# Silu read straight from PSUM for two gates of a hybrid decoder layer, one buffer doubled, one wait dropped, and all engine orders planned anew

## The reference

```python
h = rmsnorm(x, norm_g[l]) * (1.0 + scale[:, None, :]) + shift[:, None, :]
z = h @ w_in[l]
xr, gr, q, k, v, ga, qi, ki, wi = jnp.split(z, split_points, axis=-1)
xr = causal_depthwise_conv(xr, conv_w[l], conv_b[l])
y_r = rg_lru(xr, lru_wx[l], lru_bx[l], lru_wa[l], lru_ba[l], lru_a[l]) * jax.nn.silu(gr)
y_a = dsa_attention(q.reshape(B, S, N_HEADS, HEAD_DIM), k, v,
                    qi.reshape(B, S, N_IDX_HEADS, IDX_DIM), ki, wi) * jax.nn.silu(ga)
y = jnp.concatenate([y_r, y_a], axis=-1) @ w_out[l]
x = x + gate[:, None, :] * y
```

## Time and profile before

| | us |
|---|---|
| median of 3 runs | 636.92 |
| lowest, highest | 636.62, 640.52 |
| the profiled execution, device time | 639.16 |
| its span in the trace | 637.4 |
| PE busy | 540.3 (85%) |
| DVE busy | 444.1 (70%) |
| ACT busy | 374.0 (59%) |
| POOL busy | 247.5 (39%) |

### The profile page before, as it was taken

How to read it: one execution, slowest core, us unless ns; L and a number is a source line. 1 busy time by engine, 2 the same in 40 slices (tenths; PEclk the granted TensorE clock), 3 DMA queues, 4 the chain that set the end, 5 groups by cost and what they waited for, 6 DMA issues and landing times. The chain is left out here.

```text
span 637.4 us, 8051 instructions
## 1 busy us (share of the span) xinstructions
PE 540.3 (85%) x2676; PEld 447.9 (70%) x2676; DVE 444.1 (70%) x996; ACT 374.0 (59%) x678; POOL 247.5 (39%) x207
## 2 busy tenths in 40 slices
PE   2369989979999996999999406478999999999994
PEld 2356868768777773888777305467888999988873
DVE  5985467767998978945778988856456665665532
ACT  7423236544698989865789334464556675656631
POOL 5050853252525466277656400750223030304322
PEclk9859989999999999899999855559999999999999
DMA  8966460341021121035450420030010001011011
GB/s 344 411 204 230 103 152 11 99 100 32 2 66 34 34 64 35 2 99 133 117 148 2 171 93 0 0 99 2 1 67 34 33 2 67 23 45 67 0 67 66
DMA packets 16457, 51.96 MB, mean 82 GB/s; under 512 B 4000, under 2 KB 5024, under 8 KB 15392
## 3 DMA queue, kind: packets, MB, share of 16 engines
q1 hardware_dynamic: 16416, 51.45, 25.6%
HBM read 37.81 MB, written 4.19 MB: 66 GB/s over the span
## 5 line engine op out<-in xcount | busy, mean ns | idle before, releaser
L1384 PE MATMUL pair<-h_hi,w_hi 128*128 128x512 f32 (+1 forms) x352 | 115.7, 411 | 7.7 <-DVE rnn_gr L1187 4.8
L1384 PE MATMUL pair<-h_lo,w_hi 128*128 128x512 f32 (+1 forms) x352 | 111.1, 397 | 0.0
L1384 PE MATMUL pair<-h_hi,w_lo 128*128 128x512 f32 (+1 forms) x352 | 110.1, 394 | 0.0
L1309 DVE TENSOR_TENSOR pt_lo<-pair,pt_hi 128x512 fp32r<-128x512 f32 (+3 forms) x96 | 50.5, 553 | 70.6 <-ACT pt_hi L968 70.2
L863 ACT ACTIVATE bias_sb<-score_sb,tinies 128x1024 bf16<-128x1024 f32 (+2 forms) x93 | 95.7, 1033 | 2.5 <-DVE tinies L1114 2.3
L1384 PEld LDWEIGHTS pair<-h_hi,w_hi 128*128 128x128 f32 (+1 forms) x352 | 65.7, 191 | 25.9 <-issue 13.8
L692 POOL TENSOR_SCALAR w_hi<-w_raw 128x1024 fp32r<-128x1024 f32 (+1 forms) x22 | 26.9, 1223 | 137.8 <-PE pair L1384 122.1
L1384 PEld LDWEIGHTS pair<-h_lo,w_hi 128*128 128x128 f32 (+1 forms) x352 | 66.8, 190 | 16.0 <-issue 1.1
L1384 PEld LDWEIGHTS pair<-h_hi,w_lo 128*128 128x128 f32 (+1 forms) x352 | 66.6, 189 | 15.7 <-issue 0.8
L1100 DVE TENSOR_SCALAR_CACHE_REDUCE bias_sb<-score_sb,tinies 128x640 bf16<-128x640 f32 (+2 forms) x93 | 72.5, 801 | 0.9
L782 POOL TENSOR_TENSOR x_res<-q_free,x_res 128x512 f32<-128x512 f32 x14 | 18.2, 1297 | 120.3 <-DVE q_free L1280 120.3
(11 more groups left out here) (199 smaller groups left out, 1258.9 us busy)
## 6 DMA issues: line engine op xcount, KB each, us to landing
w_raw<-in_w_tiles SPq DMA_DIRECT2D x21, 512.0 KB, 3.6
ada<-in_ada_w SPq DMA_DIRECT2D x8, 1024.0 KB, 18.1
x_sb<-in_x SPq DMA_DIRECT2D x8, 512.0 KB, 6.7
ada_g<-in_ada_w SPq DMA_DIRECT2D x8, 512.0 KB, 4.5
qs<-half_hi SPq DMA_DIRECT2D x16, 256.0 KB, 3.6
qs<-half_lo SPq DMA_DIRECT2D x16, 256.0 KB, 4.4
wo_raw<-in_w_out SPq DMA_DIRECT2D x8, 512.0 KB, 6.7
x_res<-in_x SPq DMA_DIRECT2D x8, 512.0 KB, 3.4
```

The source lines that it names most:

```text
L1309: nc.vector.tensor_tensor(pt_lo[:, 4 * b:4 * b + nc4, hh, :], psum[use % 2][:, 0:nc4 * P].rearrange("p (c q) -> p c q", q=P), f32(pt_hi[:, ...
L1384: ins = nc.tensor.matmul(psum[banks[half]][0:width, :], w[b][:, k, 0:width], hh[:, k, half * HALF:(half + 1) * HALF], start=(k == 0 and p ...
```

## The change

Six edits. (1) `silu(gr)`: one ACT instruction Silu from PSUM into a buffer `gr0` or `gr1` by turns; `tg` and DVE's `grm` are gone, and what waited for `grm` (the PE tile two later, POOL's `yr`) waits for the ACT instruction. (2) `silu(ga)`: one ACT instruction instead of two on ACT and three on POOL. (3) The read-out of q tiles no longer waits for the stacking DMAs of the tile before; POOL, which then fills the buffers that these DMAs read, still waits. The read-out of q0 no longer waits for the gate's bias. (4) Read-outs into `raw`, and the gate bias DMA, wait for the last DVE step of the recurrence instead of POOL's last `yr`. (5) The costs of the planner and its rule for activation tables. (6) Hence new orders on all engines; the multiset of the other instructions is unchanged.

```diff
-COUNT_A_US = (1.35, 1.25, 1.15)
+COUNT_A_US = (1.38, 1.27, 1.16)
...
+UPDATE_LAG = 0.8
+TABLE = {"silu": "silu", "sig": "sigmoid", "decay": "sigmoid", "root": "sqrt"}
...
-            add("ACT", ("silu", c), 2.4, 2, done, ("grm", c - 1) if c else ("gacc", KC - 1))
-            add("DVE", ("grm", c), 1.3, 2, ("silu", c), *prev)
+            add("ACT", ("silu", c), 1.1, 2, done, ("yr", c - 2) if c >= 2 else ("gacc", KC - 1))
...
-                if kind == "ga":
-
-                    link(nc.gpsimd.tensor_scalar(raw[:, :], raw[:, :], 0.5, 0.5, ALU.mult, ALU.add))
-                    nc.gpsimd.tensor_tensor(ga[:, n, 0:HALF], ga[:, n, 0:HALF], raw[:, 0:HALF], ALU.mult)
-                    nc.gpsimd.tensor_tensor(ga[:, n, HALF:], ga[:, n, HALF:], raw[:, HALF:], ALU.mult).then_inc(ga_ok, 1)
...
-                    pool.wait_ge(grm_ok, ct + 1)
-                    nc.gpsimd.tensor_tensor(yr[:, ct, :], yr[:, ct, :], rnn["gr"][:, :], ALU.mult).then_inc(rnn_done, 1)
+                    pool.wait_ge(silu_ok, ct + 1)
+                    nc.gpsimd.tensor_tensor(yr[:, ct, :], yr[:, ct, :], rnn[f"gr{ct % 2}"][:, :], ALU.mult).then_inc(rnn_done, 1)
...
                     if kind == "q" and n == 0:
                         act.wait_ge(v_ps, 1)
-                        act.wait_ge(gate_ok, 1)
                 if kind in RAW_KINDS and J["gr", 0] < j:
+                    act.wait_ge(rnn_dve, 5 * CT)
+                if kind == "ga":
                     act.wait_ge(rnn_done, CT)
                 if kind == "kv":
                     act.wait_ge(slot_done, IDX_SLOTS)
-                if kind in ("qi", "q"):
+                if kind == "qi":
                     act.wait_ge(stacked, 64 * QS.index(j))
...
-                    nc.scalar.activation(ga[:, n, :], src[:, :], ACT.Copy)
-                    ins = nc.scalar.activation(raw[:, :], src[:, :], ACT.Tanh, scale=0.5)
+                    ins = nc.scalar.activation(ga[:, n, :], src[:, :], ACT.Silu)
...
-                    if o[1]:
-                        act.wait_ge(grm_ok, o[1])
+                    if o[1] >= 2:
+                        act.wait_ge(rnn_done, o[1] - 1)
                     else:
                         act.wait_ge(gacc_ok, KC)
-                    nc.scalar.activation(tg, pairs[J["gr", o[1]] % 2][:, :], ACT.Sigmoid).then_inc(silu_ok, 1)
+                    nc.scalar.activation(rnn[f"gr{o[1] % 2}"][:, :], pairs[J["gr", o[1]] % 2][:, :], ACT.Silu).then_inc(silu_ok, 1)
...
-                    nc.vector.tensor_tensor(rnn["gr"][:, :], pairs[J["gr", ct] % 2][:, :], tg, ALU.mult).then_inc(grm_ok, 1)
...
-                            pe.wait_ge(grm_ok, ct + 1)
+                            pe.wait_ge(silu_ok, ct + 1)
```

More of the change, by code:

```diff
@@ L80 @@
 BIAS_OFF = {i: sum(keys_of(t) for t in range(i)) for i in range(NT)}
-RAW_KINDS = ("kiwi", "qi", "ga", "kv", "q")
+RAW_KINDS = ("kiwi", "qi", "kv", "q")
 RAW_USE = [j for j, t in enumerate(TILES) if t[0] in RAW_KINDS]
 EVAC = {j: n for n, j in enumerate(j for j, t in enumerate(TILES) if t[0] not in ("xr", "gr"))}
-HALVES = [j for j in RAW_USE if TILES[j][0] != "ga"]
 QS = [j for j in RAW_USE if TILES[j][0] in ("qi", "q")]
@@ L138, in stages @@
                     before = TILES[j - 2][:2]
-                    need.append({"xr": ("conv", before[1], 3), "gr": ("grm", before[1])}.get(before[0], ("evac", j - 2)))
+                    need.append({"xr": ("conv", before[1], 3), "gr": ("silu", before[1])}.get(before[0], ("evac", j - 2)))
             if j or k:
@@ L143, in stages @@
         done = (("kstep", j, STEPS[j] - 1), 0.2)
-        rnn_free = [("yr", c) for c in range(CT) if J["gr", c] < j]
+        rnn_free = [("rnn", c, 4) for c in range(CT) if J["gr", c] < j]
         if kind not in ("xr", "gr"):
@@ L156, in stages @@
                 need.append(("idx", len(UNITS) - 1))
-            add("ACT", ("evac", j), {"gate": 1.05, "kv": 3.1, "q": 1.05}.get(kind, 2.1), 3, *need)
+            if kind == "ga":
+                need.append(("yr", CT - 1))
+            add("ACT", ("evac", j), {"gate": 1.05, "kv": 3.1, "q": 1.05, "ga": 1.05}.get(kind, 2.1), 3, *need)
             need = [("evac", j)]
@@ L164, in stages @@
                 need.append(("vlo",))
-            add("POOL", ("after", j), {"ga": 3.7, "qi": 2.7, "q": 3.9}.get(kind, 2.4), 3, *need)
+            if kind != "ga":
+                add("POOL", ("after", j), {"qi": 2.7, "q": 3.8}.get(kind, 2.45), 3, *need)
         if kind in ("kiwi", "kv"):
@@ L187, in stages @@
             add("ACT", ("decay", c), 3.7, 2, (("sig", c, 1), 0.0), *([("rnn", c - 1, 4)] if c else []))
-            add("ACT", ("root", c), 2.4, 2, (("decay", c), 0.0))
-            for step, (us, after) in enumerate(((1.3, [("root", c)]), (1.3, [("root", c)]), (0.8, []), (1.3, [("pool_gx", c)]), (2.3, []))):
+            add("ACT", ("root", c), 1.15, 2, (("decay", c), 0.0))
+            for step, (us, after) in enumerate(((1.3, [("root", c)]), (1.3, [("root", c)]), (0.8, []), (1.3, [(("pool_gx", c), 0.3)]), (2.4, []))):
                 add("DVE", ("rnn", c, step), us, 3, *after, *([(("rnn", c, step - 1), 0.1)] if step else []))
-            add("POOL", ("yr", c), 2.5, 2, ("rnn", c, 4), ("grm", c))
+            add("POOL", ("yr", c), 2.5, 2, ("rnn", c, 4), ("silu", c))
     for w in range(NW):
@@ L229, in stages @@
             add("ACT", ("count_a", it, c), COUNT_A_US[c], 6, ("sign",), *([("update", it - 1, c)] if it else []))
-            add("DVE", ("update", it, c), UPDATE_US, 1, ("count_a", it, c), ("prep",))
+            add("DVE", ("update", it, c), UPDATE_US, 1, (("count_a", it, c), UPDATE_LAG), ("prep",))
         for c in range(3):
@@ L248, in stages @@
     slots = []
+    table = [""]
     todo = list(work)
@@ L266, in stages @@
         engine, us = work[event][:2]
+        if event[0] in TABLE or event[0] == "evac" and TILES[event[1]][0] == "ga":
+            us += 1.3 * (table[0] != TABLE.get(event[0], "silu"))
+            table[0] = {"decay": "exp"}.get(event[0], TABLE.get(event[0], "silu"))
         end[event] = free[engine] = start + us
@@ L418, in layer_kernel @@
         rnn = {}
-        for n, name in enumerate(("gr", "xc", "th")):
+        for n, name in enumerate(("gr0", "xc", "th", "gr1")):
             rnn[name] = sb("rnn_" + name, R_GA + 4096 * n, [P, S])
-        tg = sb("tg", R_GA + 12288, [P, S])[:, :]
         for n, name in enumerate(("gx", "a", "s")):
@@ L517, in layer_kernel @@
         silu_ok = sem("silu_ok")
-        grm_ok = sem("grm_ok")
         gx_ok = sem("gx_ok")
@@ L639, in _ @@
             sp.wait_ge(bias_ok, len(PICK))
-            sp.wait_ge(ga_ok, 4)
+            sp.wait_ge(halves_ok, len(RAW_USE))
+            sp.wait_ge(evac_done, len(EVAC))
             for ti in range(2):
@@ L822, in evacuate @@
                     if r:
-                        last = RAW_USE[r - 1]
-                        if TILES[last][0] == "ga":
-                            act.wait_ge(ga_ok, TILES[last][1] + 1)
-                        else:
-                            act.wait_ge(halves_ok, HALVES.index(last) + 1)
+                        act.wait_ge(halves_ok, r)
                     if kind == "qi" and n == 0:
```

20 lines of the change are left out of this document (7 added, 13 removed).

## The result

| | before | after |
|---|---|---|
| median of the runs timed side by side | 637.83 us | 620.73 us |
| lowest to highest | 636.62 to 640.52 | 619.93 to 621.56 |
| profiled execution, and its span | 639.16, 637.4 | 619.93, 618.1 |

The changed kernel takes 0.9726 of the time of the one before, with an interval of 0.969 to 0.9763. The forecast was 618.4 with a range of 614 to 626, so the time fell into the range, 2.3 us above the forecast. The span of the profiled execution came out at 618.1 where 617.9 had been worked out.

A forecast was written before the change was run, and what follows sets the result against it. DVE's own counts were taken to bound the phase before the loop, PE next. own_thr 19.5 us earlier took 639.16 to 619.7, less 2.2 for the median gave 617.4, plus 1 for waits 618.4; range 614 to 626.

The forecast's parts named there:

- What bounds: Before the loop: DVE's own counts end the phase, late through waits for ACT; without these and grm, own_thr at 338.3.
- TensorE: PE from gate0 to the projection's end: kv0 does not wait, k-steps take 1.36 us, end at 345.9 instead of 357.68.
- ACT and DVE up to kv0: At ct 3: square root ends at 257.2, eight counts bring ACT to 265.4, kv0 is read out until 268.5.
- The q tiles: POOL waits for stacking DMAs instead of ACT; splits at 283, 293.6, 304.2; costs ACT 1 to 3 us at q2, q3.
- The tail: End of the search: ga2 at 335.0, eight counts 8.2 us plus 0.3, post 5.8, own_thr at 353.3 instead of 372.79.
- Lock-step (A): Search rounds on ACT and DVE: each waits for the other, nothing overlaps, time 625.5 us; 15 in 100.
- ACT dearer (B): On ACT: table switches or Silu cost twice their rows, time 622 to 623 us; 8 in 100.
- POOL's wait (C): Stacking waits hold POOL's slab splits, so PE waits: 643 us and more, 3 in 100; 631 to 643, 4 in 100.
- (D): Loop's start: search ends earlier but w_out or the clock holds the start, 624 to 631 us; 3 in 100.

The follow-up runs named there:

- e7: Kernel before the change, ordered with planner costs set to the intervals seen in the trace; 631.8 us, ratio 0.9889.
- e10: Changed kernel with ga tiles done as before (copy and tanh on ACT, sigmoid and product on POOL), planned with matching costs; 623.2 us, ratio 0.9763.
- e8: Changed kernel with one gr buffer instead of two, the planner told of the resulting wait; 624.7 us, ratio 0.9784.
- e4: Changed kernel with only planner costs changed, to the intervals between instruction starts seen in the trace; 607.4 us, ratio 0.9523.
- e2: Changed kernel with ACT's wait for the stacking DMAs put back ahead of q tile read-outs; 624.5 us, ratio 0.9793.
- e9: Changed kernel with two POOL slab splits moved later, behind the last yr and behind q0's split; 631.7 us, ratio 0.9889.

## Why the prediction was right, point by point

**What bounds: held.** "DVE's own counts end the phase": the stretch from `own_thr` to the end of the span is 264.9 here and 264.6 before, and every gain or loss of the start of the loop came out in the time. It is 264.3 to 265.5 in the other runs but e7 (266.9, the masks beside ga3) and e10, where `post` ended the search and not DVE's own counts. But I let TensorE's stalls do much of the explaining. In e8 TensorE stalls 5.9 us at kv0 and the whole single buffer costs 4; in e4 TensorE ends 4.3 us later than in after (351.48 against 347.16) and the time is 13 us less. What matters is how full ACT and DVE are.

**TensorE: the mechanism held, three terms were missing.** From gate0 to the first scores I had 101.2 us (345.9 less 244.67); it took 103.6. The transposes waited 1.2. The k-steps behind gate0 and behind the gates took 1.73 (244.95 to 246.68 in the timeline) and 1.79 (249.38 to 251.17) instead of 1.36, 0.8 together; some 0.4 is left of small terms. The kernel also arrived at gate0 1.1 earlier than I assumed, which hides half of it. That was luck: DVE's first count too is 1.2 earlier than before, and such starts differ by up to 2.7 between profiles. The Silu, taken from the nearest row, was right at 1.02, and the first load was done before gr3 was.

**ACT and DVE up to kv0: too early by 1.7.** The square root was to end at 257.2 and did (256.12 + 1.06). kv0's read-out was to end at 268.5 and ended at 270.2. This is the step that I left out: I priced the recurrence by its rows and POOL's split by its rows, and did not look at whether the two would lie on top of each other now. They did, for 1.1 us on DVE, and the last step ended at 267.05. Without it ACT would have read kv0 from about 266, as its own eight counts ended at 265.9 and not at 265.4, 0.5 of it a wait for an update; the other 0.6 of the 1.7 is there.

**The q tiles: held.** POOL waits for the stacking (three waits, the longest 4.2). The q0 to q2 splits, expected to be done by 283, 293.6 and 304.2, have their stackings issued at 283.0, 293.6 and 305.2. ACT waited 3.4 at q2 and 2.4 at q3, where I had 1 to 3 for the waiting on POOL; the part that POOL alone caused is 0.8 and 1.4. e2 put the value of the dropped wait at 4 us.

**The tail: held, with errors that cancel.** ga2 came at 336.5 instead of 335.0, the eight counts behind it took 8.0 instead of 8.5, `post` 5.3 instead of 5.8 (one of its small steps takes 0.17 here and took 0.66 before). `own_thr` came at 353.21 for 353.3, 6.1 behind the last k-step, where up to 8 had been given.

**The rivals.** Lock-step (A) did not come: DVE's waits for counts fell to 9.6. But it was not nothing: e4 took 8.6 of those away and with them 13 us, so this order lies between full overlap and lock-step, and I had no means of pricing that from the order. ACT dearer (B) fell: the loads cost 1.28 each, 14 of them from 190 to 345 us, and Silu cost what the sigmoid did. By the Trainium skill, "ScalarE: Activation LUTs", section "What ACT_TABLE_LOAD costs", a drain of 1.38 would have come with each; the trace shows the next instruction 1.30 after the load's start, and ahead of the load at 252.36 an instruction that ends at 252.34, and the measurement decides. POOL's wait (C) did not hold a split by itself; in e9 a split begun 11.5 us later made TensorE wait 2.2 at q1. (D) fell, the stretch behind `own_thr` being the same.

**Which part was worth what.** Taking one thing out of the changed kernel and planning anew costs: the second buffer 3.7 us, the stack wait's removal 4.3 (without a new plan), the new costs 3.4, Silu for ga 2.4 (much of it the collision seen in e10); each by its ratio less 0.9726, times 638, and each uncertain by about 2. They sum to 13.8 of 17.5. The 3.7 that are left are not the price of one part: the Silu for gr, which takes the product off DVE, and the waits moved from `yr` to the last DVE step were not run alone, and e4 with e7 shows that gains here do not simply add.
